# Prompt norm inside the sample chunk, first products around the last projection, key pages loaded during attention, keys turned between value products

## The reference, cut to what matters

```python
u = _rms(x, norm_mix)
(dn_qkv, dn_z, dn_b, dn_a, r_q, ..., a_q, a_k, a_v, i_q, i_k, i_w, gate) = _split_cols(u @ w_in)
# branch A: gated DeltaNet
c, dn_conv_new = _causal_conv(dn_qkv, dn_conv0, dn_conv_w)
q, k, v = split(silu(c));  q = _l2norm(q) * DN_DK**-0.5;  k = _l2norm(k)
o_a, dn_s_new = _chunked_recurrence(q, k, v, g, beta, dn_s0)
o_a = _rms(o_a, dn_norm) * silu(dn_z)          # the norm over the 128 values of a head
# branch B: retention; branch C: sparse attention over the keys that an indexer selects
o_c = attend(a_q, a_k, a_v, i_q, i_k, i_w)     # the sample part reads paged cache_k / cache_v
h = x + (sum over the branches of sigmoid(gate_i) * (branch_i @ w_branch_i)) @ w_o
y = h + ConvFFN(_rms(h, norm_ffn))
```

## Time and profile before

| | us |
|---|---|
| median of three runs | 3038.18 (3035.11 to 3042.14) |
| the profiled execution | 3036.19 |
| its span, first to last instruction | 3034.3 |
| PE busy | 2817.3 (93% of the span) |
| DVE, ACT, POOL busy | 1620.5, 1177.2, 788.7 |
| mean granted clock of PE | 0.955 of full speed |

### The profile page before, as it was taken

How to read it: one execution, slowest core, us unless ns; L and a number is a source line. 1 busy time by engine, 2 the same in 40 slices (tenths; PEclk the granted TensorE clock), 3 DMA queues, 4 the chain that set the end, 5 groups by cost and what they waited for, 6 DMA issues and landing times. The chain is left out here.

```text
span 3034.3 us, 56732 instructions
## 1 busy us (share of the span) xinstructions
PE 2817.3 (93%) x22451; PEld 2635.6 (87%) x22451; DVE 1620.5 (53%) x2513; ACT 1177.2 (39%) x2049; POOL 788.7 (26%) x364
## 2 busy tenths in 40 slices
PE   5998999998999799999979989999899979999998
PEld 4998888887887799999968989888888869999997
DVE  2363665564445549558225538546644464781861
ACT  3442333673223533333334315447622343432332
POOL 1221131221002333343322203222200124334431
PEclk8999899999999899999979979999999999999998
DMA  5221333534335432232242223255343344223323
GB/s 173 70 84 51 104 103 96 171 120 123 110 99 178 141 84 80 68 104 80 68 117 70 70 67 99 97 150 159 108 119 104 109 152 151 70 71 104 84 74 95
DMA packets 371700, 316.74 MB, mean 104 GB/s; under 512 B 47726, under 2 KB 321544, under 8 KB 370502
## 3 DMA queue, kind: packets, MB, share of 16 engines
q10 hardware_dynamic: 257332, 188.09, 20.9%
q1 hardware_dynamic: 114098, 124.96, 14.1%
HBM read 276.84 MB, written 36.15 MB: 103 GB/s over the span
## 5 line engine op out<-in xcount | busy, mean ns | idle before, releaser
L873 POOL TENSOR_TENSOR w_lo<-w_raw,w_hi 128x1024 fp32r<-128x1024 f32 (+2 forms) x360 | 788.5, 2194 | 2207.9 <-ACT w_hi L1564 2207.7
L880 PE MATMUL big<-uhi,w_hi 128*128 128x272 f32 x4096 | 1242.3, 303 | 54.0 <-DVE ulo L2084 31.9
L882 PE MATMUL big<-uhi,w_lo 128*128 128x272 f32 x4096 | 1200.6, 293 | 0.0
L881 PE MATMUL big<-ulo,w_hi 128*128 128x272 f32 x4096 | 1195.1, 292 | 0.0
L880 PEld LDWEIGHTS big<-uhi,w_hi 128*128 128x128 f32 x4096 | 788.5, 192 | 108.2 <-issue 60.1
L881 PEld LDWEIGHTS big<-ulo,w_hi 128*128 128x128 f32 x4096 | 789.9, 193 | 4.2 <-issue 1.9
L882 PEld LDWEIGHTS big<-uhi,w_lo 128*128 128x128 f32 x4096 | 787.5, 192 | 0.0
L1564 ACT ACTIVATE w_hi<-w_raw 128x1024 fp32r<-128x1024 f32 (+2 forms) x360 | 343.7, 955 | 425.1 <-PE big L882 329.5
L880 PE MATMUL big<-hhi,w_hi 128*128 128x272 f32 x704 | 205.9, 292 | 3.9 <-DVE hlo L2664 3.9
L882 PE MATMUL big<-hhi,w_lo 128*128 128x272 f32 x704 | 203.5, 289 | 0.0
L881 PE MATMUL big<-hlo,w_hi 128*128 128x272 f32 x704 | 202.7, 288 | 0.0
(11 more groups left out here) (360 smaller groups left out, 3905.2 us busy)
## 6 DMA issues: line engine op xcount, KB each, us to landing
w_raw<-in_w_in ACTq DMA_DIRECT2D x66, 1024.0 KB, 5.6
w_raw<-in_w_up ACTq DMA_DIRECT2D x88, 512.0 KB, 5.0
kpage<-in_cache_k SPq DMA_DIRECT2D x128, 256.0 KB, 3.1
w_raw<-in_w_down ACTq DMA_DIRECT2D x32, 704.0 KB, 4.7
d_conv<-in_cache_v SPq DMA_DIRECT2D x64, 256.0 KB, 2.7
d_pad<-in_cache_v SPq DMA_DIRECT2D x64, 256.0 KB, 2.7
gate_dram<-gate_raw ACTq DMA_DIRECT2D x48, 272.0 KB, 2.5
w_raw<-in_w_branch ACTq DMA_DIRECT2D x24, 512.0 KB, 3.7
```

Of the source, the lines that this page charges most:

```text
L873: po.tensor_tensor(split_view(lo, t), tile_of(t), split_view(hi, t).bitcast(F32), ALU.subtract).then_inc(w_lo.sem, w_lo.next(t))
L880: pe.matmul(out, wh, xh, start=start, stop=False)
L881: pe.matmul(out, wh, xl, start=False, stop=False)
L882: return pe.matmul(out, wl, xh, start=False, stop=stop)
```

## The change

Four edits in the layer program.

- **Keys** are turned inside the value tiles: PE turns key chunk c between the halves of value tile c, and chunk 4 behind the tiles. The values are then turned through aux 1, 2 and 3 in rotation, and DVE, not ACT, copies them out; ACT sends the rows.
- **Key pages** 0 to 2 have buffers of their own place, and SP loads them without waiting for the attention to end; PE turns pages 0 and 1 between its last products of attention. DVE builds `s_q` ahead of the attention.
- **First chunk**: `grow`, `betarow` and `kq` of chunk 0 are issued ahead of and inside the last projection tile, `kk` behind it, with their DVE and ACT steps; the sample value product moves from aux 1 to aux 2.
- **Norm**: the prompt's 512 columns are normalised in chunk 4, through big 1, aux 2 and aux 3, and the 32 sample columns within the first of the rounds. The 16 branch tiles then stand 16 steps at the start of chunk 4 and 8 steps, not 4, in each round.

```diff
 SP
+        for i in range(NPAGES):
+            if i == KFIRST:                      # KFIRST = 3
-        sp.wait_ge(PJ[0].drained, PJ[0].at(('ao', 3)))
+                sp.wait_ge(PJ[0].drained, PJ[0].at(('ao', 3)))
...
 PE
+        for h in range(H):
+            dense_tile(('av', h), h % 2, f'av{h // 2}', h % 2, g.uhi, g.ulo, between=lambda: turn_heads(h))
+        turn_heads(4)
         pe.wait_ge(PJ[1].drained, PJ[1].at(('av', 3)))
         for c in range(5):
-            turn(X[0], ('kT', c), P, n, [g.akv[:, h, cs] for h in range(H)], P)
-            turn(X[1], ('vT', c), P, n, [g.akv[:, 4 + h, cs] for h in range(H)], P)
+            turn(X[1 + c % 3], ('vT', c), P, n, [g.akv[:, 4 + h, cs] for h in range(H)], P)
...
+            if i == len(steps):
+                turn_keys(0)
+                turn_keys(1)
...
                 if p == SELECT_AT + 3:
                     new_values()
+                    gate_rows(0, X[0], 'betarow')
+                    pe.wait_ge(vec_out.sem, vec_out.at(('l2', 7)))
+                    key_products(0, X[3], 'kq')
...
             if p == SELECT_AT + 2:
                 sample_probabilities()
+                gate_rows(0, X[1], 'grow')
+        key_products(0, X[2], 'kk')
...
-            if c == 4:
-                advance(branches, 8)
...
-                advance(branches, 8)
+                for bank, key, heads in ((PJ[1], ('pvar', 0), (0, 1)), (X[2], ('pvar', 2), (2,)), (X[3], ('pvar', 3), (3,))):
+                    pe.wait_ge(bank.drained, bank.claim(key))
+                    for i, h in enumerate(heads):
+                        pe.wait_ge(act_out.sem, act_out.at(('psq', h)))
+                        mm = pe.matmul(bank.ap[:, i, :] if len(heads) > 1 else bank.ap[:, :], ones, g.d_sq[:, h, 0:SEQ],
+                                       start=True, stop=True)
+                    mm.then_inc(bank.filled, 1)
+                advance(branches, 16)
...
                     advance(branches, 4)
-        advance(branches, 4)
-        pe.wait_ge(X[3].drained, X[3].at(('do', 4)))
-        for h in range(H):
-            column_sums(('dvar', h), h % 2, ...)
-            if h % 2:
-                advance(branches, 16 if h == 1 else 8)
+                    if b == 0:
+                        pe.wait_ge(X[3].drained, X[3].claim('svar'))
+                        pe.wait_ge(act_out.sem, act_out.at('ssq'))
+                        pe.matmul(head_view(X[3].ap, n), ones, g.d_sq[:, :, SEQ:NT], start=True, stop=True).then_inc(
+                            X[3].filled, 1)
+                    advance(branches, 4)
...
 DVE, chunk 4
             update(c, n, levels[-1], 1, True)
             if c == 4:
+                for i in range(2):
+                    ve.wait_ge(act_out.sem, act_out.at(('prs', i)))
+                    norm_rows(2 * i, 2, 0, SEQ, None)
                 branch(2)
                 branch(3)
```

More of the change, by code:

```diff
@@ L845, in _ @@
         state(10)
[L846 to L854, removed]
+        for t in range(11, 16):
+            gate(t)
+            state(t)
+        for t in range(16, 19):
             gate(t)
@@ L1117, in logits, with turn_keys @@
             mm.then_inc(X[i % 2].filled, 1)
+        def turn_keys(i):
+            pe.wait_ge(k_in[i % KPAGES].sem, k_in[i % KPAGES].at(i))
+            turn(X[i % 2], ('sk', i), P, P, [g.kpage[i % KPAGES][:, h * P:h * P + P] for h in range(H)], P)
         gates = gate_steps(ATT_GATES)
@@ L1932, in _ @@
             if c == 3:
+                prompt_square(0)
+                prompt_square(1)
                 for h in range(H):
@@ L2272, in _ @@
         choose_rounds(g.sel_s, 4 * H, ROUNDS_S - 10)
+        for c in range(5):
+            bank, n = X[1 + c % 3], chunk_of(c)[1]
+            ve.wait_ge(bank.filled, bank.at(('vT', c)))
+            ve.tensor_copy(g.vtok[0:n, c, :], bank.ap[0:n, :]).then_inc(bank.drained, 1)
+            ve.wait_ge(bank.drained, bank.at(('vT', c)))
+        ve.wait_ge(PJ[1].drained, PJ[1].at(('aq', 3)))
+        ve.memset(g.s_q[:, :, :], 0.0).then_inc(vec_steps.sem, vec_steps.next())
+        ve.wait_ge(vec_steps.sem, vec_steps.count)
+        ve.tensor_copy(g.s_q[:, :, :].rearrange("p h (b n) -> p h b n", b=DB)[:, :, :, 0:DS],
+                       g.out_att[:, :, SEQ:NT].rearrange("p h (b t) -> p h b t", b=DB)).then_inc(
+            vec_out.sem, vec_out.next('s_q'))
+        ve.wait_ge(vec_out.sem, vec_out.count)
         steps = [(qb, h) for qb in range(4) for h in range(H)]
@@ L2348, in sample_logits, with gate_steps_of @@
             ve.wait_ge(vec_out.sem, vec_out.count)
+        def gate_steps_of(c):
+            n = chunk_of(c)[1]
+            ve.wait_ge(X[1].filled, X[1].at(('grow', c)))
+            x = X[1].ap
+            for h in range(H):
+                ts(g.d_dec[0:n, h * n:h * n + n], x[0:n, h * n:h * n + n], gC[0:n, c, h:h + 1], 0.0,
+                        ALU.subtract, ALU.min).then_inc(vec_out.sem, vec_out.next(('dif', c) if h == 3 else None))
+                ve.wait_ge(vec_out.sem, vec_out.count)
         odd_pages(-1)
@@ L2430, in _ @@
             tri = const('triu') if c < 4 else const('triu_s', NS)[:, 0:NS]
[L2431 to L2436 removed]
+            if c:
+                gate_steps_of(c)
             ve.wait_ge(act_out.sem, act_out.at(('dec', c)))
```

220 lines of the change are left out of this document (116 added, 104 removed).

## The result

The changed kernel took 2994.57 us (median of 4 runs, 2991.63 to 2997.11), the kernel before 3037.85 (median of 4): ratio 0.9856, 95% interval 0.9842 to 0.9871. That is 43 us less. The forecast was 2997, with a range of 2977 to 3018. The profiled execution took 2997.11, its span is 2995.0; that of before was 3034.3, so the two traces to be compared differ by 39.3.

A forecast was written before the change was run, and what follows sets the result against it. PE, busy 93% of the span, was taken as the bound, gaining only where it waits or runs slowly. 5.5 + 7.2 - 3.5 + 11.6 = 20.8 us a layer, 41.6 for both, gave 2997 us, range 2977 to 3018.

The forecast's parts named there:

- Part 1: Keys turned in the value tiles: first softmax product earlier, 5.5 us a layer gained, bounds 3.5 to 7.3.
- the 7.3: Value turns to softmax: first softmax product at about 445.2 instead of 452.52, 7.3 us earlier if the clock holds.
- the alternation with PE: Value turns: DVE's five copies alternate with PE's turns, adding about 1.1 us before the softmax chain.
- Part 2: Key pages loaded in attention: first key product 7.3 us earlier, net 7.2 a layer, bounds 6 to 7.3.
- Part 3: Opening of chunk 0: products moved ahead of the last projection tile's end cost 3.5 us a layer, bounds 1 to 5.
- the fourth page moves by 2.5: Sample value pages: twelve products ahead of the last tile's end move the fourth page from 717.9 to about 720.4.
- Part 4: Norm in chunk 4: first round 10.9 us later, branch tile 16 9.6 earlier; gain 11.6 a layer, bounds 7 to 14.
- 4 of the 5.9 on DVE counted: Chunk 4: DVE's four norm steps take 5.9 us; 4 delay the first round, part lying beside PE's triangular products.
- The clock did not spread: Rival: after long idle at value pages and chunk 4, PE stays below 2.4 GHz; slower, 3056 us; chance 0.05.
- Chunk 4's price did not eat its gain: Rival: chained gate loads delay branch tiles and rounds, so the norm edit gains 0; 3020 us; chance 0.14.
- The opening did not gain: Rival: value pages land early, chunk 0's 5.6 us wait is gained instead of 3.5 lost; 2978; chance 0.10.
- All four edits did what they were to do: Rival denied: pages 0 to 2 no earlier, or softmax waits for DVE's copies; 3008 to 3011 us; chance 0.11.

The follow-up runs named there:

- exp_table_early: The changed kernel with one added single-column exponential behind the last Silu, so ACT loads that table in PE's wait at the value pages; 2998.32 us.
- opening_behind_tile: The changed kernel with the first-chunk edit alone undone: all four opening products of chunk 0 behind the last projection tile; 2989.28 us.
- two_products_behind: The changed kernel with `betarow` and `kq` of chunk 0 moved back behind the last projection tile, ahead of the first value page; 2995.43 us.
- value_pages_early: The changed kernel with the first four value pages in buffers chunk 0 uses only later, loaded once projection tile 10 is copied out; 2985.72 us.
- norm_after_gates: The changed kernel with DVE's four norm steps of 1024 columns behind branch tiles 2 and 3 and chunk 4's scaled queries; 2993.26 us.
- norm_between_rounds: The changed kernel with DVE's norm steps in two halves behind branch tiles 5 and 6; 2991.16 us.

## Why the prediction was right, point by point

**Part 1 (5.5 a layer forecast, 6.5 and 6.3 measured): right within its bounds, one reason wrong.** I had taken 2 us off the 7.3 for a slow clock; the clock there is 1.00. DVE's timeline shows where the rest of the 7.3 went:

```profile
439.59 3.58 DVE L2330 COPY vtok<-aux 128x512 f32<-128x512 f32 x5 [10.62 <-PE aux L941]
443.47 1.02 DVE L2333 MEMSET s_q<- 128x1152 f32 x1 [0.31 <-DVE vtok L2330]
444.53 0.23 DVE L2335 COPY s_q<-out_att 128x128 f32<-128x128 f32 x1
444.79 0.29 DVE L2347 TENSOR_TENSOR logit<-aux,sel 128x128 f32<-128x128 f32 x1
```

The five copies run without a gap, 0.72 each, so the alternation with PE that I added (1.1) doesn't exist. But the first of them starts 27.3 behind the last key tile's copy, which on the time scale of before is 438.3, 0.9 later than my 436.8 and a turn; and copies, memset and the copy into `s_q` take 5.2 with their gaps, where I had 4.5.

**Part 2 (7.2, measured 7.2 and 7.0, undone 7.4 and 7.0): right.** All its steps are seen: the last attention product ends at 498.13, the first key product stands at 502.15, 4.0 behind it, and the stretch has the full clock.

**Part 3 (a loss of 3.5, measured 5.2 and 5.1): sign and mechanism right, size short.** The step "the fourth page moves by 2.5" holds: the products behind the pages start at 708.50 instead of 718.23, 9.7 earlier where PE came 12.35 earlier: 2.6. The wait is 9.94, where I said 11. Undersized was what follows. The slow clock behind the wait costs 1.6 (the lead of 9.7 is 8.1 at chunk 0's copy of `d_lm`), not 1.0. And I had no term for ACT: with chunk 0's exponentials ahead of the last Silu, the table is loaded again in chunk 1, 1.0 us. exp_table_early shows that step alone, and opening_behind_tile, two_products_behind and value_pages_early show that what ends the wait is the tile's end, Silu and the transfer.

The Trainium skill, "TensorE: Matmul & The Clock Gate", section "HAM oscillation — how this bites in real kernels", says that the work behind a long wait starts cold; the trace agrees, with 0.68 granted in the 5.5 us behind the 9.94.

**Part 4 (11.6, measured 12.5 and 12.1): right, with errors that cancel on the way.** Counted from DVE's first step of chunk 4, the chain was forecast against measured as follows: first sigmoid 11.7 later, measured 10.0; `d_T` 6.9, measured 4.2; first round 10.9, measured 10.4. On ACT's timeline after, first sigmoid and copy of `d_T`:

```profile
917.15 0.66 ACT L1597 ACTIVATE gate_raw<-gate_raw 128x544 f32<-128x544 f32 x1
...
921.90 0.25 ACT L1597 ACTIVATE d_T<-aux 32x128 f32<-32x128 f32 x1
```

The logarithms and exponentials were cheaper than by columns (1.11 and about 1.0 for 1024, where two of 544 are 1.42). What I had taken off for overlap (4 of the 5.9 on DVE counted) was not there: from `d_T` to the first round it takes 6.3 longer than before, as much as the norm on DVE, 6.1 from 926.30 to 932.4. Without the norm in front only 3.5 to 3.9 come back (norm_after_gates), since PE's branch tile 3 is the next wait. The first state update follows in 26.2, as before. I called the row at 1017.21 the start of branch tile 16; it is the tile's third step, where it waited. The product at that place now stands at 1000.72: 16.5 earlier, of which 7.1 were there at chunk 4, so 9.4 against 9.6 forecast. Behind it, 3.2 instead of 2 were gained: the clock is 1.00, and PE's wait ahead of the products with `w_o` is 3.9 instead of 5.5.

The Trainium skill, "ScalarE: Activation LUTs", section "Table sets: the hidden batching unit", has logarithm and exponential in one set. The trace differs: a load of 1.28 stands between them at 912.53, as the order showed.

**The sum.** By the stretches 21.0 and 20.3 a layer were gained where 20.8 were forecast. That it fits so well is in part luck: in the first layer the parts are off by 1.0, 0, -1.7 and 0.9, and these errors cancel.

**The rivals.** The clock did not spread. From the products behind the pages to chunk 4 it is 0.99 against 1.00, all of it in the 5.5 us behind the wait; in chunk 4 up to the first round it is 0.80 against 0.87, and from the first update to branch tile 16 it is 1.00 against 0.91. Chunk 4's price did not eat its gain. The opening did not gain. All four edits did what they were to do, as each undone part shows.

## What to carry to other kernels

Before work is moved out of a wait, ask what ends that wait. If what ends it is a chain that starts at the work just ahead, products moved in front of it cost their full time, and those left behind it are free; the same 8 products cost 1.7 us or nothing.
An engine that an edit loads more holds up what is queued behind it on other engines too: here a norm on DVE reached PE through a gate load and the state loads behind it in SP's queue.
A change that gains 43 us can hold a part that loses 10 in its own stretch; undoing each part by itself shows it, if it is read from landmark to landmark: a start alone and one execution's span also carry what happened elsewhere.

## What the runs showed of the hardware

DVE's products of two operands and 1024 columns (line 2491) took 1.22 or 2.18 us in the same kernel. The slow ones fall together with a POOL instruction. POOL's and DVE's timelines of the changed kernel:

```profile
926.41 2.31 POOL L872 TENSOR_TENSOR w_lo<-w_raw,w_hi 128x512 fp32r<-128x512 f32 x1 [4.95 <-ACT w_hi L1597]
```

```profile
926.30 1.28 DVE L2489 SCALAR_TENSOR_TENSOR qkv<-qkv,par 128x1024 f32<-128x1024 f32 x1
927.62 2.18 DVE L2491 TENSOR_TENSOR x<-x,qkv 128x1024 f32<-128x1024 f32 x1
929.83 1.28 DVE L2489 SCALAR_TENSOR_TENSOR qkv<-qkv,par 128x1024 f32<-128x1024 f32 x1
931.15 1.22 DVE L2491 TENSOR_TENSOR x<-x,qkv 128x1024 f32<-128x1024 f32 x1
```

POOL's own instruction takes 2.31 there, against 1.28 at the same place in norm_after_gates, whose norm meets no POOL work and takes 1.22 to 1.23 for all four of these products in the run. In opening_behind_tile and two_products_behind both products of each layer meet POOL and take 2.17 to 2.25; the one more that is slow costs about 1.0, half to two thirds of what those two kernels give back in chunk 4 up to the first round, and the rest stays open. In norm_between_rounds the order is the other way round: POOL starts first and keeps its 1.30, and DVE's product of line 2489, begun 0.27 later, takes 2.10 instead of 1.28.

```profile
950.39 1.30 POOL L872 TENSOR_TENSOR w_lo<-w_raw,w_hi 128x512 fp32r<-128x512 f32 x1 [3.25 <-ACT w_hi L1597]
```

```profile
950.66 2.10 DVE L2489 SCALAR_TENSOR_TENSOR qkv<-qkv,par 128x1024 f32<-128x1024 f32 x1
```

That the two engines take turns is read from these rows, and no run tested it by itself. The Trainium skill, "SBUF — State Buffer", section "SBUF: two separate sides", describes an exclusive lock between GpSimd and a DVE instruction with two operands in SBUF; the rows agree with it.
